# First mixer of a two-block transformer kernel: split slots of the compression weights, and the order of constants, window blocks and value copies

## The reference, cut to what matters

```python
def _even_mixer(h, w_in, a_conv, a_i_b, a_f_b, a_norm, b_cmp_pos, b_cmp_w1, b_cmp_w2, b_g_b, w_out):
    aq, ak, av, ao, ai, af, bq, bkc, bvc, bks, bvs, bkw, bvw, bg = _split(h @ w_in, EVEN_SIZES)
    ya = _mlstm(aq, ak, av, ao, ai + a_i_b, af + a_f_b, a_conv, a_norm)
    yb = _nsa(bq, bkc, bvc, bks, bvs, bkw, bvw, bg + b_g_b, b_cmp_pos, b_cmp_w1, b_cmp_w2)
    return jnp.concatenate([ya, yb], -1) @ w_out

def compress(u, j):
    blk = u[:, win] + cmp_pos[j][None, None, :, None, :].astype(dt)   # windows of 32 tokens, stride 16
    blk = blk.transpose(0, 1, 3, 2, 4).reshape(B, M, B_KV, B_CMP_LEN * B_DH)
    return jax.nn.gelu(blk @ cmp_w1[j]) @ cmp_w2[j]

k_cmp = compress(r(kc_raw), 0)
v_cmp = compress(r(vc_raw), 1)

# in _mlstm: the rows of the gates, by chunks
b = jnp.cumsum(lf, axis=-1)                        # lf = log_sigmoid of the forget gate
D = jnp.where(causal, b[..., :, None] - b[..., None, :] + ic[..., None, :], NEG)
m_t = jnp.maximum(m_inter, D.max(-1))
```

## Time and profile before

| | |
|---|---|
| median of 3 runs | 3480.68 us (3476.71 to 3483.46) |
| profiled execution, its own time | 3482.01 us |
| span of the profiled execution | 3480.7 us, mean granted TensorE clock 0.975 |
| TensorE products busy | 3294.6 us (95%) |
| TensorE weight loads busy | 2898.8 us (83%), beside the products |
| VectorE, ScalarE, GpSimd busy | 2008.5 (58%), 1472.8 (42%), 1027.1 us (30%) |
| DMA | 308.98 MB, mean 89 GB/s |
| chain that ended last | TensorE 74%, VectorE 18%, ScalarE 4%, issue 2% |

### The profile page before, as it was taken

One profiled execution on the slowest core, in us unless ns is written; L12 is line 12 of the kernel. 1 busy time (PEld: TensorE's weight loads), 2 busy tenths in 40 slices (PEclk: granted clock), 3 DMA queues, 4 the chain that ended last, 5 costly groups with the idle time before them and its releaser, 6 DMA issues.

```text
span 3480.7 us, 47895 instructions
## 1 busy us (share of the span) xinstructions
PE 3294.6 (95%) x20092; PEld 2898.8 (83%) x20092; DVE 2008.5 (58%) x3021; ACT 1472.8 (42%) x2258; POOL 1027.1 (30%) x459
## 2 busy tenths in 40 slices
PE   7898999999879999998999999999999999999999
PEld 6686789987655899977999877999999998789998
DVE  4457555463682744446565544855685566358556
ACT  3454344444332454435344322544454443325333
POOL 2220123332420133321332432233313333322232
PEclk9999999999889999999999999999999999999999
DMA  3310323331110233221342322233313423222232
GB/s 126 100 49 1 97 85 110 101 111 55 55 43 25 91 108 111 100 94 55 110 127 71 124 85 85 60 117 122 110 49 121 127 74 120 73 86 90 91 111 77
DMA packets 239816, 308.98 MB, mean 89 GB/s; under 512 B 8337, under 2 KB 168097, under 8 KB 239089
## 3 DMA queue, kind: packets, MB, share of 16 engines
q1 hardware_dynamic: 236016, 291.41, 26.1%
q0 software_dynamic: 3584, 14.52, 1.2%
HBM read 303.80 MB, written 2.10 MB: 88 GB/s over the span
## 4 chain that ended last, share of the span: by engine, by line
PE 74%; DVE 18%; ACT 4%; issue 2%; DMA 0%; POOL 0%; DVEq 0%; ACTq 0%
PE bank L585 23%; PE bank L587 23%; PE bank L586 22%; DVE wlo L1995 2%; ACT whi L1269 1%; PE bank L605 1%; DVE wraw L2017 1%; DVE wkk_o L2798 1%; ACT P_e L1581 1%; DVE raw_w L2017 1%; PE bank L1112 1%; DVE gb L2795 1%; DVE uv_x L2929 1%; DVE h L2037 1%; DVE h L2050 1%
## 5 line engine op out<-in xcount | busy, mean ns | idle before, releaser
L3053 POOL TENSOR_TENSOR wlo<-wraw,whi 128x1024 fp32r<-128x1024 f32 (+3 forms) x246 | 631.5, 2570 | 1483.7 <-ACT whi L1269 1483.3
L585 PE MATMUL bank<-xh,whi 128*128 128x256 f32 (+1 forms) x2456 | 721.9, 294 | 42.8 <-DVE xl L2270 12.4
L1269 ACT ACTIVATE whi<-wraw 128x1024 fp32r<-128x1024 f32 (+3 forms) x426 | 440.3, 1038 | 722.8 <-PE bank L587 585.1
L587 PE MATMUL bank<-xh,wlo 128*128 128x256 f32 (+1 forms) x2456 | 716.6, 292 | 0.0
L586 PE MATMUL bank<-xl,whi 128*128 128x256 f32 (+1 forms) x2456 | 713.2, 290 | 0.0
L3053 POOL TENSOR_TENSOR wlo<-raw_w,whi 128x1024 fp32r<-128x1024 f32 (+1 forms) x148 | 357.2, 2416 | 766.7 <-ACT whi L1269 766.7
L585 PEld LDWEIGHTS bank<-xh,whi 128*128 128x128 f32 x2456 | 465.3, 189 | 61.1 <-POOL wlo L3053 24.7
L585 PE MATMUL bank<-whi,uh_w 128*128 128x512 f32 x1216 | 474.6, 390 | 0.0
L586 PEld LDWEIGHTS bank<-xl,whi 128*128 128x128 f32 x2456 | 465.7, 190 | 10.5
L587 PE MATMUL bank<-whi,ul_w 128*128 128x512 f32 x1216 | 473.5, 389 | 0.0
L586 PE MATMUL bank<-wlo,uh_w 128*128 128x512 f32 x1216 | 473.4, 389 | 0.0
(11 more groups left out here) (400 smaller groups left out, 5259.8 us busy)
## 6 DMA issues: line engine op xcount, KB each, us to landing
wraw<-in_w_in SPq DMA_DIRECT2D x26, 1024.0 KB, 5.1
wraw<-in_ffn_w_down SPq DMA_DIRECT2D x20, 1024.0 KB, 5.1
raw_w<-in_ffn_w_down SPq DMA_DIRECT2D x20, 1024.0 KB, 5.1
raw_w<-in_mlp_w SPq DMA_DIRECT2D x19, 1024.0 KB, 5.3
wraw<-in_mlp_w SPq DMA_DIRECT2D x17, 1024.0 KB, 5.3
wraw<-in_ffn_w_gate SPq DMA_DIRECT2D x32, 512.0 KB, 4.6
raw_w<-in_ffn_w_gate SPq DMA_DIRECT2D x32, 512.0 KB, 4.9
raw_w<-in_ffn_w_up SPq DMA_DIRECT2D x32, 512.0 KB, 5.0
```

The costliest lines, as they stand in the source:

```text
L585: M.matmul(o, lh, rh, start=start, stop=False, skip_group_check=more)
L587: return M.matmul(o, ll, rh, start=False, stop=stop, skip_group_check=more)
L1269: A.activation(hi, raw, ACT.Copy).then_inc(*k.w_hi.inc(("hi", j)))
L3053: G.tensor_tensor(lo[:, 0:n], raw[:, 0:n], hi[:, 0:n].bitcast(F), ALU.subtract).then_inc(*k.w_lo.inc(("lo", j)))
```

## The change

It does five things, all in the first mixer:

1. `cmp` items get no halves; they have an empty `before`.
2. TensorE's wait for `cmb` moves from ahead of the gate product to ahead of `memory()`.
3. VectorE makes the constants and the two clears after the first two of the four `e_in` pairs; the window additions of block 0 come between the third and the fourth pair, those of block 1 after the fourth.
4. ScalarE's four `e_vs` copies move from behind the gate rows' chain to ahead of it, right after the copies of the gate rows.
5. VectorE looks ahead once more (`slots.prepare()`) ahead of its part of the gate rows' chain.

```diff
@@ slot
+        if tag == "cmp":
+            self.items.append(Item(tag, self.loads[load], [], [], 0, nk, "none"))
+            self.loads[load].items = [len(self.items) - 1]
+            return
...
-            self.loads[load].items = [self.item(tag, load, 2, 0, nk, "both" if share and tag != "cmp" else "pool")]
+            self.loads[load].items = [self.item(tag, load, 2, 0, nk, "both" if share else "pool")]
@@ tensor_program, even
         pe.wait_ge(at("con"))
-        pe.wait_ge(at("cmb"))
...
+        pe.wait_ge(at("cmb"))
         units = memory()
@@ scalar_program, even
         A.activation(e.r_f, bank[64:68, :], ACT.Copy).then_inc(*done.inc(("r_f",), ("free", ("e_g",))))
+        def e_vs(key, tt):
+            copy_out(key, e.vsw[:, tt, :, :, 0, :], ring.of(key)[:, 0:256].rearrange("p (a g d) -> p a g d", a=2, g=2), ("vsw one", tt))
+        run(tm_units("e_vs", ("e_vs",), e_vs))
         act.wait_ge(at("r_f bias"))
...
         A.activation(e.r_em, e.r_b, ACT.Exp, scale=-1.0).then_inc(*done.inc(("r_em",)))
-
-        def e_vs(key, tt):
-            copy_out(key, e.vsw[:, tt, :, :, 0, :], ring.of(key)[:, 0:256].rearrange("p (a g d) -> p a g d", a=2, g=2), ("vsw one", tt))
-        run(tm_units("e_vs", ("e_vs",), e_vs))
         act.wait_ge(at("gts bias"))
@@ vector_program, even
-        fm("e_in", [[("e_in", 2 * n), ("e_in", 2 * n + 1)] for n in range(4)], e_in)
+        fm("e_in", [[("e_in", 2 * n), ("e_in", 2 * n + 1)] for n in range(2)], e_in)
         dve.wait_ge(at("con"))
...
         for n in range(2):
+            V.memset(e.blk[n], 0.0).then_inc(*done.inc(("windows empty", n)))
+
+        def windows(n):
             blk = e.blk[n]
-            V.memset(blk, 0.0).then_inc(*done.inc())
-            dve.wait_ge(done.now())
+            dve.wait_ge(at("windows empty", n))
             dve.wait_ge(at("kvT"))
...
+        fm("e_in", [[("e_in", 4), ("e_in", 5)]], e_in)
+        windows(0)
+        fm("e_in", [[("e_in", 6), ("e_in", 7)]], e_in)
+        windows(1)
         slots.skip("e_g", 1)
+        slots.prepare()
         dve.wait_ge(at("r_f"))
```

## The result

The kernel after takes 3496.7 us (median of 7), the one before, in the same rounds and three earlier runs, 3485.5 us (median of 7). The ratio is 1.0033 (95% interval 1.0023 to 1.0042): 11 us slower. The prediction said 3490.1, with a range of 3483 to 3497, from a base of 3480.7 and a loss of 9.4 us. The base itself came out 4.8 us higher in the later runs, and the loss 1.8 us larger. One execution of the kernel before, among those beside e5, e6, e8 and e9, took 8238 us; the ratios leave it out, and without it the median of 3483.6 us there is 3483.3.

What follows compares the result with a forecast made beforehand. TensorE, 95% busy, was taken as the bound, with two large stops at 60 to 100 us. Removing them won 12 us, but added ScalarE waits left +9.4 us: 3490.1 on the median, range 3483 to 3497.

Steps and rivals of the forecast that it cites:

- Where TensorE stood, and why: Stops of 5.71 us before the gate product and 10.16 us before the first qk product go, their releasers coming earlier.
- The clock after the 3.65 us stop: Slow products after TensorE's stop ahead of e_vs (sized 3.7 us) cost 1.4 us, bounds 0 and 2.0.
- The added wait: ScalarE stands before the fourth e_vs copy for item 9's data, issued after hidden(0), landing at 93.8 (91.4 to 96.5).
- The chain behind it: Gate chain, sigmoid and gelu queue on ScalarE behind that data: Abs at 96.1, hidden features ready at 109.6.
- The 0.6 for the port: VectorE's scalar addition to the gate rows, beside GpSimd's split of item 9, is held up 0.6 us.
- the bound of 1.25: Upper bound, in us, for VectorE's scalar addition waiting on GpSimd: what is left of 2.3 behind the table load.
- The second stop: Before hidden(1)'s features TensorE stands 5.2 us: ScalarE awaits item 10's data, with silu and kch ahead of gelu.
- the two clock terms: Slow products after the stop ahead of e_vs and after the 5.2 us stop, counted as 1.4 us each.
- The block behind it: After the qk group, ending at 140.1 against 130.7, the rest moves as one block: +9.4 us in all.
- (a): Rival: early work carries through if item 9's data is there at 81.7; gain gone at 87.5; 3475, chance 0.05.
- (b): Rival: later stops, such as TensorE's 3.47 us at 158.5, absorb part of the loss; 3486.6, chance 0.2.
- (c): Rival: costs of hidden(0), second load, scalar addition and last clock at upper ends; +13.8, so 3494.5, chance 0.15.

Runs made afterwards that it cites:

- e5: Kernel after, with ScalarE looking ahead to item 10 only behind gelu of hidden(1): 3485.3 us against 3483.6 for the kernel before, ratio 1.0003.
- e6: Kernel after, looking ahead to item 9 only behind gelu of hidden(0) and to item 10 only behind gelu of hidden(1): 3475.2 us, ratio 0.9976 to before.
- e8: Kernel before, with fifty more gelu activations on ScalarE ahead of the real one of hidden(0): 3491.9 us against 3483.6, ratio 1.0027.
- e9: Kernel after without point 5, gate chain ahead of value copies, item 7 split inside it, look ahead to items 9 and 10 limited: 3467.2 us against 3483.6 before.
- e1: Kernel before with points 2 and 3 alone (cmb wait moved; constants, clears and windows early): 3475.5 us against 3484.7, ratio 0.9971.
- e3: Kernel after, with SyncE issuing load 9 (item 9's data) ahead of load 8: 3484.0 us against 3484.7 for the kernel before, ratio 0.9999.
- e4: Kernel after, with ScalarE's look ahead to item 9 held until gelu of hidden(0), VectorE's until the gate bias: 3479.4 us against 3484.7 before, ratio 0.9983.
- e7: Kernel after without point 1, so compression items keep their split slots: 3480.6 us against 3483.7 for the kernel before, ratio 0.9989.
- e10: Kernel after, with useless products on TensorE inside its three stops, no wait taken away: 3487.7 us against 3483.7 for the kernel before, ratio 1.0013.

## Why the prediction was right

The direction and the mechanism came out as told, and the loss is 11.2 us for 9.4. That the time itself, 3496.7, lies inside a range that ends at 3497 is partly luck: it is 6.6 us above the forecast, of which 4.8 come from the base and 1.8 from the loss.

*Where TensorE stood, and why.* Right: both stops fell away as soon as their releasers came earlier. `e_vs` started at 68.20 (68.65 predicted); this trace runs 0.5 us early from the gate product on (58.85 for 59.35), which is all of the difference.

*The clock after the 3.65 us stop.* Mis-sized. I took 1.4 us, with an upper bound of 2.0; from the start of `e_vs` to the end of `hidden(0)` were 86.45 - 68.20 = 18.2 us, 2.7 more than the 15.5 of before. `hidden(0)` ended at 86.45, outside my 84.2 to 86.2. A stop's length alone did not tell its cost: 10.16 us had cost 2.0. One trace doesn't tell it either. The same stop (3.62 to 3.65 us) stands in eight kernels; by the same difference it cost 2.6 or 2.7 us in five (after, e1, e3, e6, e9) and 1.6 in three (e4, e5, e7). The granted clock (the third number from the end) shows it, first in the kernel after, then in e5, where the stop ends at 69.23 and the slow products at 72.7:

```profile
68.20:74.10 5.90, 5.90 (x27) 5.90 (x28) 3.51 (x7) 0.59 (x1) 0.00 (x0) 0.50 0.58 178
```

```profile
69.20:72.70 3.50, 3.47 (x16) 3.47 (x17) 3.41 (x7) 0.00 (x0) 0.00 (x0) 0.53 0.64 176
72.70:82.00 9.30, 9.30 (x80) 9.30 (x80) 4.43 (x4) 2.97 (x4) 4.85 (x4) 1.00 0.13 47
```

So my 1.4 was near the lower of the two values, and the bound of 2.0 too low for the other. The prediction also passed over a stop in the earlier trace rows: behind the 5.71 us ahead of the gate product, that product took 71.93 - 65.06 = 6.9 us instead of 5.7.

*The added wait.* Right, and it is the whole sign of the result. Both loads were issued behind `hidden(0)`; the data came at 94.66 (93.8 predicted). The second load landed 7.7 us after its own issue, against 5.3 for one alone. e3 and e4 show that this wait is the cause. (My upper bound for the landing, 96.5, is 96.3 by its own terms.)

*The chain behind it.* Abs at 96.74 (96.1), features at 110.3 (109.6): 13.5 us from one to the other, as in the sum (12.9 and 0.6). The 0.6 for the port is the 0.60 us for which ScalarE waits at 99.92: VectorE's scalar addition took 1.84 us instead of 0.42, beside GpSimd's low half of item 9:

```profile
98.05 1.84 DVE L2331 TENSOR_SCALAR og_e<-og_e 4x512 f32<-4x512 f32 x1 [18.30 <-ACT og_e L1490]
```

```profile
97.27 2.34 POOL L3062 TENSOR_TENSOR wlo<-wraw,whi 128x1024 fp32r<-128x1024 f32 x1
```

It ended at 99.89 and GpSimd's at 99.61, so it stood until GpSimd was done. The rule of the Trainium skill ("SBUF — State Buffer", Who interferes with whom) holds here for the one-input form too. The price was 0.6 and not the bound of 1.25, since the addition came up 0.8 us into GpSimd's operation and the table load hid most of what was left of it. (Of that bound, 2.3 less the table load's 1.28 gives 1.0; the other 0.25 was not named.)

The prediction said that no row shows this for an operation with one input in SBUF. That is so for the rows that it shows, but the trace of before has one, far behind this stage. Beside a GpSimd operation of 2.42 us that starts at 562.46, such an operation took 2.46 us, and the next of its shape 0.26:

```profile
562.54 2.46 DVE L2546 TENSOR_SCALAR ang_w<-ang_w 128x192 f32<-128x192 f32 x1
565.04 0.26 DVE L2548 TENSOR_SCALAR ang_w<-ang_w 128x192 f32<-128x192 f32 x1
```

It bears on the term of 0.6, and the prediction did not use it.

*The second stop.* Right in kind, and e5 shows the cause by taking it away: silu and `kch` stand ahead of gelu (131.53, 132.06, 133.58), the stop is 5.32 us (5.2). The size was off in one term: the last product took from 134.20 to 142.1, 7.9 us, where I had 7.1: again the clock, 2.2 us after a stop of 5.3, not 1.4. The group ended 11.4 us late, not 9.4; the 2.0 missing are the two clock terms (1.3 and 0.8), while the smaller misses of the other terms (-0.45 at the start of `e_vs` among them) about cancel. The clock terms are the part of the sum that failed.

*The block behind it.* Right for the time, less so for one trace. In the kernel after, the profile is 13.5 us longer than before's while the group is 11.4 later. The table and e8 speak against a rule that a shift grows later: behind the product at 162 the traces are 3317 to 3329 us long (span less that start), 3319 for before, 3321 for after, with no order by what was changed ahead. What moves this tail from run to run was not looked into.

*The rivals.* (a) would have needed the data of item 9 by 87.5; e3 shows that at 84.07 the kernel is already level with before, where (a) by its own rate, a microsecond lost for each one later, would still be 3 us faster. Its sum left out ScalarE's split of item 9: it lets Abs start 0.5 us behind the data, and in e3 that takes 2.1 us (84.07 to 86.15). It also left out the wait for the port, 0.66 us in e3. (b): nothing was absorbed; TensorE's stop of 3.47 us is 3.48 in the kernel after. (c), costs at their upper ends, is the rival that came nearest, 3494.5 for 3496.7; its loss, 13.8, is further from the 11.2 measured than the forecast's 9.4.

## What to carry to other kernels

When work is put ahead of a queue by a look ahead, ask of every wait that the look ahead can now reach who issues its data and when: a slot that comes free can pull a long wait in front of urgent small work. The same slots, with a limit on the look ahead and the chain ahead of the copies, gave a kernel 16 us faster than before instead of 11 slower; some 7 of the 16 are theirs. Test the parts of a change one at a time: two of five points here were worth 9 us alone, and the rest turned them into a loss. Count a stop of the matrix engine with the slow products behind it, and take their cost as a range from several traces: the same stop cost 1.6 us in some kernels here and 2.7 in others.

## What the runs showed of the hardware that was not expected

The granted clock after a stop. The products that follow run at half of the full clock (1.2 instead of 2.4 GHz; granted 0.50 from 68.20 to 74.10 in the kernel after) for a while that the stop's length doesn't give. 2.7 us were lost after 3.65 us in the kernel after, 1.6 after the same 3.65 in e5, 2.2 after 5.32, 2.0 after 10.16. Nor does the length tell whether the clock falls at all: behind a stop of 1.73 us in the kernel before no product was slow, behind 1.99 us in e1 seven were, behind 2.74 us in e1 none, and behind 1.45 us in e10 eight. What decides it was not looked into. With the stops filled by useless products, the same kernel was 7 us closer to the one before by the medians (+4.0 instead of +11.2) and 5.3 in the traces; 2.6 and 2.2 of these are the slow products behind the first and the third stop.

Two loads one behind the other. A second load right behind another of 1 MB landed 7.7 us after its issue, 2.4 later than one alone, which fits one transfer of 2.8 us (1.05 MB at 376 GB/s) behind the other, less the 0.4 between the issues.

An operation of VectorE with one input in SBUF stood until GpSimd's operation, which had started first, was done: 1.84 us instead of 0.42 in the kernel after, 2.46 instead of 0.26 in the kernel before.
